# A down projection turned from plain matmuls into rounds of seven products

## The reference

```python
def conv_gated_mlp(h, w_gate, w_up, conv_ffn_w, conv_ffn_b, w_down):
    g = causal_dwconv(h @ w_gate, conv_ffn_w, conv_ffn_b)
    return (jax.nn.gelu(g) * (h @ w_up)) @ w_down
...
        x = x + rmsnorm(y, norm_mix_post[l])
        h = rmsnorm(x, norm_ffn_pre[l])
        y = conv_gated_mlp(h, w_gate[l], w_up[l], conv_ffn_w[l], conv_ffn_b[l], w_down[l])
        x = x + rmsnorm(y, norm_ffn_post[l])
```

## Time and profile before

| | |
|---|---|
| median of 3 runs | 2187.09 us (2187.03 to 2187.22) |
| span of the profiled execution, first to last instruction | 2186.0 us |
| what lies around the span (median less span) | 1.1 us |
| PE busy | 2171.7 us (99%) |
| DVE busy | 1529.4 us (70%) |
| ACT busy | 1002.2 us (46%) |
| POOL busy | 141.7 us (6%) |
| DMA | 329.01 MB, mean 151 GB/s |

### The profile page before, as it was taken

The page is one execution under the profiler, slowest core; times in us unless marked ns, Lnnn a source line. Parts: engine busy times, 40 slices in busy tenths (PEclk is TensorE's granted clock), DMA queues, the critical chain, the costliest instruction groups (busy, mean ns, idle before and its releaser), DMA issues.

```text
span 2186.0 us, 45684 instructions
## 1 busy us (share of the span) xinstructions
PE 2171.7 (99%) x18942; PEld 2154.4 (99%) x18942; DVE 1529.4 (70%) x2030; ACT 1002.2 (46%) x1278; POOL 141.7 (6%) x210
## 2 busy tenths in 40 slices
PE   9999999999999999999999999999999999999998
PEld 8999999999999999999999999999999999999998
DVE  7776777778755977888888888888885444444445
ACT  6555555447322554444444444444443343343433
POOL 0000000000100001111111111111111100000000
PEclk9999999999999999999999999999999999999999
DMA  5222222222432437777777777777767632222343
GB/s 175 91 99 94 85 92 95 89 96 87 150 112 97 163 116 203 209 214 210 209 203 206 209 206 207 209 214 204 204 178 219 192 113 97 96 96 96 99 170 116
DMA packets 100850, 329.01 MB, mean 151 GB/s; under 512 B 13024, under 2 KB 20832, under 8 KB 100208
## 3 DMA queue, kind: packets, MB, share of 16 engines
q1 hardware_dynamic: 75456, 240.06, 31.9%
q0 software_dynamic: 22672, 82.36, 17.5%
q10 hardware_dynamic: 2592, 4.72, 0.6%
HBM read 306.09 MB, written 21.00 MB: 150 GB/s over the span
## 4 chain that ended last, share of the span: by engine, by line
PE 97%; DVE 2%; ACT 1%; issue 0%; POOL 0%; DVEq 0%; ACTq 0%; POOLq 0%
PE bank L1816 31%; PE bank L1818 31%; PE bank L1817 31%; PE bank L1901 1%; PE bank L1914 1%; PE bank L1926 0%; DVE x_b L1807 0%; PE bank L1925 0%; PE bank L1986 0%; ACT w_all L589 0%; DVE w_all L1058 0%; PE bank L1872 0%; PE bank L2004 0%; PE bank L2003 0%; PE bank L1932 0%
## 5 line engine op out<-in xcount | busy, mean ns | idle before, releaser
L1816 PE MATMUL bank<-act_hi,w_all 128*128 128x256 f32 x2832 | 786.3, 278 | 1.7 <-DVE act_lo L1530 0.9
L1818 PE MATMUL bank<-act_hi,w_all 128*128 128x256 f32 x2832 | 782.2, 276 | 0.0
L1817 PE MATMUL bank<-act_lo,w_all 128*128 128x256 f32 x2832 | 782.1, 276 | 0.0
L1816 PEld LDWEIGHTS bank<-act_hi,w_all 128*128 128x128 f32 x2832 | 531.6, 188 | 5.4 <-issue 2.5
L1817 PEld LDWEIGHTS bank<-act_lo,w_all 128*128 128x128 f32 x2832 | 531.7, 188 | 0.4
L1818 PEld LDWEIGHTS bank<-act_hi,w_all 128*128 128x128 f32 x2832 | 531.6, 188 | 0.0
L1816 PE MATMUL bank<-w_all,act_hi 128*128 128x256 f32 x1536 | 424.0, 276 | 0.1
L1818 PE MATMUL bank<-w_all,act_lo 128*128 128x256 f32 x1536 | 423.9, 276 | 0.0
L1817 PE MATMUL bank<-w_all,act_hi 128*128 128x256 f32 x1536 | 423.9, 276 | 0.0
L1068 DVE TENSOR_TENSOR w_all<-raw,w_all 128x1024 fp32r<-128x1024 f32 x95 | 116.4, 1226 | 279.5 <-ACT w_all L595 279.5
L1816 PEld LDWEIGHTS bank<-w_all,act_hi 128*128 128x128 f32 x1536 | 288.3, 188 | 0.3 <-issue 0.3
(11 more groups left out here) (297 smaller groups left out, 3707.0 us busy)
## 6 DMA issues: line engine op xcount, KB each, us to landing
raw<-weights SPq DMA_DIRECT2D x310, 512.0 KB, 3.3
raw_s<-weights SPq DMA_DIRECT2D x84, 512.0 KB, 5.0
raw_s<-weights POOLq DMA_DIRECT2D x84, 512.0 KB, 5.7
raw_a<-weights SPq DMA_DIRECT2D x42, 512.0 KB, 5.5
h_spill<-h_out POOLq DMA_DIRECT2D x48, 256.0 KB, 3.4
h_t<-h_spill POOLq DMA_DIRECT2D x24, 512.0 KB, 4.1
x<-xT POOLq DMA_DIRECT2D x16, 256.0 KB, 3.9
out<-x ACTq DMA_DIRECT2D x16, 256.0 KB, 2.3
```

The costliest lines, as they stand in the source:

```text
L1816: pe.matmul(dst, ah, bh, start=start, stop=False, skip_group_check=goes_on)
L1817: pe.matmul(dst, ah, bl, start=False, stop=False, skip_group_check=goes_on)
L1818: return pe.matmul(dst, al, bh, start=False, stop=stop, skip_group_check=goes_on)
```

## The change

The down projection becomes 24 more rounds of the seven-product loop (rounds 42 to 65): three blocks of 16 hidden tiles (`CH = 3`), and in each block eight pairs of output tiles (`PAIRS_OUT = 8`). The moving operands are now quadrants and sums of `h`.

- In the hidden stage DVE makes the sums of each pair of `h` tiles (`t_of_pair`, `t3_of_pair`), and POOL stores all seven operands to `t_spill` in rows of 256 floats (`store_pair`, `store_t3`), in place of one store of 128 x 512 per tile.
- At each block's start its seven operands of 128 x 2048 floats (1 MB each) are loaded (`load_t`, POOL), split by ACT (`t_n_hi`) and DVE (`t_n_lo`) between the splits of the weights: operand 0 after product 5 of the round before the last, operands 1 to 6 after six weight splits in a row (`T_AFTER`), starting at product 5 of the last round.
- The weights keep their layout in DRAM, so A11, A12 and A22 of a down round are loaded as 1024 pieces of 128 floats. S1 and S3 are made ahead in DRAM (`w_sums`): for each of the 24 rounds two copies and two adding DMAs from DRAM to DRAM, 96 in all, issued by POOL in the mix stage; SP then loads the sums plainly.
- Partial outputs of block 0 are stored to `y_parts` (two tiles of 256 KB per round), those of block 1 are added there by the DMA, and in block 2 they are loaded back and DVE adds to them in place.
- The output has channels on the partitions, so the end needs no transposes: one root and one spread over the partitions, then DVE scales 16 tiles, and DVE (4 tiles) and POOL (12 tiles) add the residual.

The core of the diff:

```diff
+            def sums(n0, n1):
+                for n in range(n0, n1):
+                    if n:
+                        pool.wait_ge(s_added, 32 * n)
+                    copy_for_sums(n)
+                    add_for_sums(n)
+
+            sums(0, 2)
+            for p in range(1, NP):
                 pool.wait_ge(gw_split, p)
-                pool.dma_start(gw[:], gate_w[bass.ds(p, 1)].rearrange("a p m n -> p (a m) n")).then_inc(gw_landed, 16)
+                pool.dma_start(gw[:], gate_w[p]).then_inc(gw_landed, 16)
                 pool.wait_ge(s_taken, p * 6)
...
+                sums(3 * p - 1, 3 * p + 2)
+            sums(3 * NP - 1, ND)
...
+            def load_t(c, n):
+                pool.wait_ge(unit_used, t_free_after(c, n))
+                m = CK * (c + 1)
+                for stored_t, each in ((to_stored, 16), (te_stored, 16), (tq_stored, 32), (t3_stored, 16)):
+                    pool.wait_ge(stored_t, each * m)
+                pool.dma_start(operand(NS + PAIRS_OUT * c, n)[3], t_d[c, T_PLACE[n]].rearrange("p (k n) -> p k n", n=HS)).then_inc(t_landed[n], 16)
...
+            for i in range(NF):
+                if i <= NS:
+                    store_after(PLAIN - 1 + i)
+                elif i == NS + 1:
+                    store_t3(HT - 1)
                 if i + 1 < NS:
                     add_to_s3(i + 1)
                 if i + 2 < NS:
                     add_to_s1(i + 2)
...
+                c, o = (i + 1 - NS) // PAIRS_OUT, (i + 1 - NS) % PAIRS_OUT
+                if i > NS and i - 1 < NS + 2 * PAIRS_OUT:
+                    store_y(i - 1)
+                if i >= NS - 2 and c + 1 < CH and o == PAIRS_OUT - 1:
+                    load_t(c + 1, 0)
+                if i >= NS - 1 and c < CH and o == 0:
+                    for n in range(1, 6):
+                        load_t(c, n)
+                    if c == CH - 1:
+                        load_y(0)
+                        load_y(1)
+                    load_t(c, 6)
...
+            def t_n_after(i, n, convert):
+
+                k = 7 * (i - (NS - 1)) + n
+                for c in range(CH):
+                    if k == 7 * PAIRS_OUT * c - 2:
+                        convert(c, 0)
+                    for m in range(1, 7):
+                        if k == 7 * PAIRS_OUT * c + T_AFTER[m]:
+                            convert(c, m)
...
-            for g in range(GROUPS):
-                n, out_banks = g * PER_GROUP, DOWN_BANKS[g % 2]
...
-                with pe.Fori(1, PER_GROUP // 2 - 1) as t:
-                    down_unit(t * 2 + n, 0, out_banks)
-                    down_unit(t * 2 + (n + 1), 1, out_banks)
```

More of the change, by code:

```diff
@@ L96 @@
 LINE = 64
-H_STEP = 2 * S + 6 * LINE // 4
 LOG1P = [1.0 / n for n in (15, 13, 11, 9, 7, 5, 3)]
@@ L1805, in _ @@
-            for k in range(KT):
-                dve.wait_ge(lifted, k + 1)
-                dve.scalar_tensor_tensor(out=x1_b[:, k], in0=banks[k % 8][:], scalar=col("g_ffn_post", k),
-                                         in1=x1_b[:, k], op0=ALU.mult, op1=ALU.add).then_inc(taken, 1)
+                if i <= NS:
+                    t_after(j - 1)
+                if square >= 0:
+                    add_y_square(square + 1)
+                lo(i, 5)
+                stage_free(i)
+                c22_of(i)
@@ new lines, in _ @@
+            dve.wait_ge(x1_back, 16 * KT)
+            dve.wait_ge(spread_done, 5)
+            for t in range(KT):
+                y = Y_TILES[t]
+                dve.scalar_tensor_tensor(out=y, in0=y, scalar=col("g_ffn_post", t), in1=banks[1][:], op0=ALU.mult,
+                                         op1=ALU.mult).then_inc(z_done, 1)
+                if t in ADD_BY_DVE:
+                    dve.wait_ge(z_done, t + 1)
+                    dve.tensor_tensor(x1_place(t), x1_place(t), in_two(y), ALU.add).then_inc(taken_d, 1)
@@ L1872, in channel_sum @@
                     last = pe.matmul(bank[:], ones[:], src, start=(i == 0), stop=(i == len(srcs) - 1))
-                last.then_inc(sum_done, 1)
-            def column_sum(bank, src):
-                for j in range(QT):
-                    last = pe.matmul(bank[:, j:j + 1], src[:, P * j:P * j + P], ones[:, 0:1], start=True, stop=True)
                 last.then_inc(sum_done, 1)
@@ L2298, in _, with column_sums @@
-            for k in range(4, KT):
-                at_least(pe, taken, k - 7)
-                for i in range(QT):
-                    last = lift(k, i)
-                last.then_inc(lifted, 1)
+                fast_product(i, 5, c, False)
+                fast_product(i, 6, b, False)
+            def column_sums(src, j0, j1, stop):
+                for j in range(j0, j1):
+                    last = pe.matmul(banks[0][:, j:j + 1], src[:, P * (j - j0):P * (j - j0) + P], ones[:, 0:1],
+                                     start=src is acc and j == 0, stop=stop, skip_group_check=True)
+                return last
```

793 lines of the change are left out of this document (426 added, 367 removed).

## The result

The changed kernel takes 2195.07 us (median of 6 runs, 2193.20 to 2196.22), the kernel before 2187.11 (6 runs beside them, 2186.86 to 2187.22). The ratio is 1.0035 (95% interval 1.0024 to 1.0047): slower by 8.0 us, where 13 us faster was forecast. The profiled execution took 2196.11 us, its span is 2194.3.

A forecast was written before the change was run, and what follows sets the result against it. The prediction took PE, busy for 99% of the span, as the bound, so time follows the matmul count. 2187.1 - 65.2 (576 fewer matmuls) + 46 (block changes) + 5 (mix stage) + 1 (tail) = 2174 us, range 2155 to 2182.

The forecast's parts named there:

- first change: Block change in rounds 40 to 42: 11 us from POOL's queue, 7 from operand 1, 8 from DVE; 26 us.
- second: Second block change: 6 us of DVE work beyond the round and some 2 us of late loads; 8 us.
- third: Third block change: the second's 8 us plus 4 for two y loads ahead of `pu_done` in round 58; 12 us.
- mix stage: Weight sums in POOL's queue delay `gw`, so ACT and PE wait: +5 us at 17.7 us per sum, bounds 0 and 250.
- hidden stage: Added pair sums and stores fit DVE's free time and a round's cover: no cost, up to 5 us without that cover.
- tail: After the last product: 22 us against 20.4, +1; if POOL's addition takes 2 us instead of 1.1, +8.
- the sum of the block changes: All three operand changes in the down projection: +46 us, bounds +31 and +80.
- DVE's surplus: DVE's work beyond the 19.0 us rounds at the block changes, from six 2.2 us conversions: 8, 6 and 6 us.
- the line's 20.4: Mix stage: price in us of one weight sum, from a line through the times of 4 KB and 1 KB pieces.
- The rival of a stretched mix stage: Mix stage: DRAM-to-DRAM additions take over 21.6 us per sum; 2218 at 23, 2258 at 25; chance 0.34 (over 2191).
- It cancels: First `gw` late by 11 us and block changes of 54 to 60 give 2187; chance 0.10 (2183 to 2191).
- covered changes of 15 to 30: Rival: block changes mostly covered, costing 15 to 30 us, no mix stall: 2138 to 2155; chance 0.14 (under 2155).

The follow-up runs named there:

- e2: The changed kernel without the three changes of operands (no loads of h sums, conversions or PE waits for them; y loads stay): 2136.68 us.
- e1: The kernel before with the 24 weight sums added to POOL's queue in the mix stage, read by nothing: 2188.34 us.
- e6: The changed kernel with operand 0's load a round earlier and the loads of operands 1 to 3 ahead of t3's store: 2176.99 us.
- e14: e3 with half-bank additions and p1's copy put ahead of the conversions: 2158.20 us.
- e13: The changed kernel with only half-bank additions and p1's copy put ahead of the conversions, loads as late as they were: 2183.39 us.
- e9: e6 with half-bank additions and p1's copy put ahead of the conversions: 2161.71 us.
- e7: The changed kernel with y's first two tiles put into gb and cv and loaded ahead of the third change's operands: 2197.72 us.
- e15: e3 with 36, 24 and 33 matmuls into an unread bank ahead of PE's wait for pu in rounds 42, 50 and 58: 2163.07 us.
- e4: The changed kernel with 100 and 65 matmuls into an unread bank ahead of PE's waits before product 5 of rounds 40 and 41: 2194.93 us.
- e3: The changed kernel with all conversions kept but the 21 loads of h sums left out; y loads stay: 2168.01 us.

## Why the prediction was wrong, point by point

The forecast was 2174, and 21 us are missing from it.

| term | forecast | measured |
|---|---|---|
| matmuls removed | -65.2 | -65.2: e2 shows full windows at the old pace |
| first change | 26 | 32.4 |
| second | 8 | 8.5 |
| third | 12 | 21.2 |
| mix stage | 5 | 0.2 in the trace, 0.9 in e1 (-1.1 to 2.8) |
| hidden stage | 0 | about 3, and some 2 that I can't place |
| tail | 1 | 6.2 |
| sum | -13 | +8 |

- **The step that failed is the sum of the block changes**, 46 for 62; it was inside its bounds of 31 to 80. The mechanism of the first (POOL's order in rounds 40 and 41) was right: 12.6 us for the forecast 11 and 8.5 for 7, and e6 takes 18 of them away. DVE's surplus was right as well: 9.0, 5.6 and 7.1 in e14 for 8, 6 and 6. What was missing is the coupling of the two through DVE's order. The forecast asked what stands behind a conversion for operand 0 in round 40 and for no other. Everywhere else it added DVE's work and the loads' lateness as if they were apart. The order alone is worth 11.7 us (e13), 9.8 without loads (e14) and 15.3 with early ones (e9).
- **The third change** was the most undersized (12 for 21), and its terms were wrong in kind. The 4 us for `y` were no term of their own: DVE doesn't wait for `y`, earlier loads of it (e7) leave PE a wait of 5.6 us, and e13 takes that wait from 7.2 to 1.7 with the loads where they were. What the change costs is DVE's surplus (7.1 in e14), late operands (3.2 more in e9) and the order (some 11, the rest).
- **The clock** had no term. It is worth 4.9 us in e15, but at the first change of the changed kernel filled gaps gave nothing (e4), so no part of the 16 us is shown to be the clock's.
- **The mix stage** went near the forecast's price per sum: 19.1 on average, between the 17.7 taken and the line's 20.4. The rule of the Trainium skill's page "DMA: Bandwidth & Descriptors" (Why small descriptors are slow) gave an estimate of some 17 for a sum (16.2 by the forecast's own terms); the trace's average of 19.1 is above it. Two errors in the stall cancelled. Two sums ahead of `gw` were counted whole, 35.4 us; POOL goes on when the additions are issued, so `gw` left 27.1 us after 66.79. But behind the sums it took 10 us to land and not the 2.3 of the earlier trace rows. ACT was 3.5 us late for the 5 forecast. What failed in this term is that the lateness reaches the end: 0.16 us of it was left at the last `gw`. The rival of a stretched mix stage, to which most of the 0.34 for slower went, did not happen: the sign came out on its side for another reason.
- **The hidden stage** at nothing: the cover in the fast rounds is there (443 or 444 matmuls per 50 us), but I did not look at the plain stage, where the same slots are used with no round between.
- **The tail**: POOL's addition was 1.1 in my sum and is 1.39 (4.17 us for three), and the end follows POOL: 16.5 us from the start of the first to the end of the last of twelve, 4.1 from there to the span's end. The alternative in the text (+8 at 2 us) had the mechanism.
- The rival *It cancels* had part of the shape: changes of 54 to 60 give most of the gain back. Its own terms add to 2188 to 2194 and not to 2187. The 11 us of a late `gw` in them did not come, and 11 of tail and hidden stage, which it had at 1 and nothing, stood in their place.
- Three numbers of the working don't follow from its rows, and none decided: 1 KB pieces are 18% slower than 4 KB ones by the earlier trace rows and not 30%; the fixed 0.17 us a piece behind the bound of 33 us for a sum comes from no row; covered changes of 15 to 30 end at 2153 and not 2155.

## What to carry to other kernels

When work is added to an engine that serves another in order, don't only compare its sum with the room: write down, for each operation that the other engine waits for, what now stands ahead of it. Here moving a few short operations ahead of long ones was worth 10 to 15 us, and alone it turned a loss of 8 us into a gain of 3.7. A wait that names an addition says which operation came last, not which input of it was late: look at what stood ahead of it. Put a load where its place comes free and not where its turn in the queue comes. Price a gap of PE above its length (three gaps of 11 us together gave back 4.9 us when filled in e15), unless something else is late behind it (e4).

## What was not expected of the hardware

- DMAs from DRAM to DRAM that add in 512-byte pieces ran beside the mix stage's weight loads at a DMA share of 0.88 (100 to 500 us) without delaying PE (3454 matmuls there, 3458 before): two copies and two additions of 512 KB in 16.4 to 22.8 us, 19.1 on average.
- Adding on POOL and DVE at once slows both. The groups of the tail in the changed kernel: one POOL addition takes 1.26 us alone or beside DVE's scaling and up to 1.72 beside DVE's addition, and one of DVE's takes 0.80 to 1.46 us, where an addition of the same shape (L1957) takes 0.68 at a time when POOL adds nothing.

```profile
L2013 DVE SCALAR_TENSOR_TENSOR tsum_f<-tsum_f,par,bank 128x512 f32<-128x512 f32 x8 | 5.4, 738 | 1.3 <-PE bank L2443 1.3
...
L715 POOL TENSOR_TENSOR tsum_f<-tsum_f,up 128x512 f32<-128x512 f32 x1 | 1.7, 1721 | 0.0
...
L2017 DVE TENSOR_TENSOR tsum_f<-tsum_f,h_out 128x512 f32<-128x512 f32 x1 | 1.5, 1457 | 0.0
L1957 DVE TENSOR_TENSOR acc<-acc,sq 128x512 f32<-128x512 f32 x2 | 1.4, 682 | 0.0
```

  The Trainium skill's "SBUF — State Buffer" (Who interferes with whom) says that a DVE instruction with two inputs in SBUF contends with a GpSimd instruction that reads SBUF, and one with a single such input doesn't; the trace agrees: DVE's scaling, whose second operand comes from a PSUM bank, keeps its 0.74 us, its additions don't.
- The granted clock fell to 0.50 in the window behind the gap of 12.6 us, to 0.56 behind that of 8.5 us, and to 0.57 behind the 4.3 us gap of e3.
